# First loads in the order of their use, x modulated in two halves of the channels, first blocks projected over half of the channels in between

## The reference

```python
m = silu(c) @ w_ada + b_ada          # -> shift1, scale1, gate1, shift2, scale2, gate2, 1024 each
h = x * (1 + scale1) + shift1
P = h @ w_in                         # one projection, cut into the inputs of two branches and gates
A = gated_delta_rule(conv(P[...]))   # starts from the state of the last 3 rows
B = rwkv7(token_shift(P[...]))       # starts from the state of the last row
mix = (sigmoid(P_gA) * (A @ p_a) + sigmoid(P_gB) * (B @ p_b)) @ w_o
x = LN(alpha * x + (1 + gate1) * mix)
x = LN(alpha * x + (1 + gate2) * MoE(x * (1 + scale2) + shift2))   # 64 experts, top 8, one shared
```

## Time and profile before

| | |
|---|---|
| median of 3 runs | 1683.13 us (1680.92 to 1695.8) |
| the profiled execution | 1685.42 us |
| its span, first to last instruction | 1683.7 us |
| busy: PE, DVE, ACT, POOL | 1430.7, 581.4, 263.0, 243.8 us |
| mean granted TensorE clock | 0.888 of full speed |
| DMA | 318.39 MB, mean 189 GB/s |

### The profile page before, as it was taken

The page is one execution under the profiler, slowest core; times in us unless marked ns, Lnnn a source line. Parts: engine busy times, 40 slices in busy tenths (PEclk is TensorE's granted clock), DMA queues, the critical chain, the costliest instruction groups (busy, mean ns, idle before and its releaser), DMA issues.

```text
span 1683.7 us, 21034 instructions
## 1 busy us (share of the span) xinstructions
PE 1430.7 (85%) x8007; PEld 930.3 (55%) x8007; DVE 581.4 (35%) x1400; ACT 263.0 (16%) x543; POOL 243.8 (14%) x281
## 2 busy tenths in 40 slices
PE   4889999686848997998898898899998889988866
PEld 1545555584637965975445465555555555555532
DVE  0423476446453334223335422222222122221107
ACT  2121441210011111221002111111111111111100
POOL 5000000030003201500000022212222122222200
PEclk9998899688867998999987999889999898998978
DMA  9364410301021011003334249899999989999854
GB/s 322 105 249 171 150 50 2 79 1 40 11 79 47 1 51 50 1 1 132 129 116 178 90 177 357 306 363 354 346 392 363 351 329 342 392 357 358 314 219 187
DMA packets 105488, 318.39 MB, mean 189 GB/s; under 512 B 22319, under 2 KB 39299, under 8 KB 88234
## 3 DMA queue, kind: packets, MB, share of 16 engines
q1 hardware_dynamic: 90694, 289.01, 46.7%
q0 software_dynamic: 12000, 25.20, 4.6%
q10 hardware_dynamic: 2692, 2.79, 0.5%
HBM read 304.53 MB, written 26.58 MB: 197 GB/s over the span
## 4 chain that ended last, share of the span: by engine, by line
PE 67%; DMA 18%; DVE 8%; issue 2%; SPq 2%; ACT 2%; POOLq 0%; DVEq 0%; POOL 0%; ACTq 0%
DMA MT<-h_rows,slot_ids 14%; PE bank L1928 13%; PE bank L1464 9%; PE bank L1587 5%; PE bank L1938 4%; PE bank L1913 3%; PE bank L1648 3%; PE bank L1837 3%; PE bank L1805 3%; PE bank L1661 3%; PE bank L1658 2%; PE bank L2026 2%; DVE inv L876 2%; DVE ring L876 2%; PE bank L1919 2%
## 5 line engine op out<-in xcount | busy, mean ns | idle before, releaser
L1928 PE MATMUL bank<-ring,MT 128*64 128x256 f32 x2400 | 324.1, 431 | 0.0
L1928 PEld LDWEIGHTS bank<-ring,MT 128*64 128x64 f32 x2400 | 187.6, 156 | 108.4 <-issue 42.1
L1351 DVE SCALAR_TENSOR_TENSOR gate<-zs,slot_gate,bank 128x128 f32<-128x128 f32 x75 | 26.1, 348 | 378.1 <-ACT zs L850 378.1
L1464 PE MATMUL bank<-hT,ring 128*128 128x384 f32 x416 | 146.2, 515 | 7.3 <-DVE hT L876 5.1
L430 POOL DMA_INDIRECT MT<-h_rows,slot_ids x75 | 71.5, 953 | 499.2 <-PE bank L1913 294.1
L1938 PE MATMUL bank<-inv,rwp 128*64 128x512 f32 x600 | 141.5, 592 | 0.4 <-ACT rwp L852 0.4
L1913 PE MATMUL bank<-ident,MT 64*128 64x64 f32 x600 | 82.9, 286 | 59.8 <-DMA MT<-h_rows,slot_ids 59.4
L1464 PEld LDWEIGHTS bank<-hT,ring 128*128 128x128 f32 x416 | 83.7, 203 | 67.4 <-issue 10.8
L1913 PEld LDWEIGHTS bank<-ident,MT 64*128 64x128 f32 x600 | 71.8, 200 | 63.9 <-DMA MT<-h_rows,slot_ids 63.1
L1587 PE MATMUL bank<-hT,ring 128*128 128x384 f32 x256 | 89.6, 510 | 10.3 <-DMA ring<-in_w_in_dram 10.3
L1587 PEld LDWEIGHTS bank<-hT,ring 128*128 128x128 f32 x256 | 50.4, 200 | 44.3 <-DMA ring<-in_w_in_dram 10.4
(11 more groups left out here) (364 smaller groups left out, 1849.1 us busy)
## 6 DMA issues: line engine op xcount, KB each, us to landing
ring<-in_we_gate_dram SPq DMA_DIRECT2D x64, 1024.0 KB, 9.0
ring<-in_we_up_dram SPq DMA_DIRECT2D x64, 1024.0 KB, 11.7
inv<-in_we_down_dram SPq DMA_DIRECT2D x64, 1024.0 KB, 8.0
ring<-in_w_ada_dram SPq DMA_DIRECT2D x12, 2048.0 KB, 14.4
ring<-in_w_in_dram SPq DMA_DIRECT2D x7, 2048.0 KB, 9.2
ring<-y_rows SPq DMA_DIRECT2D x6, 2048.0 KB, 8.1
ring<-in_w_in_dram SPq DMA_DIRECT2D x9, 1024.0 KB, 5.2
xs<-in_x_prompt_dram SPq DMA_DIRECT2D x2, 1024.0 KB, 17.0
```

Source lines behind the costliest of these rows:

```text
L1464: last = mm(bank[4 + n % 4][:, 0:T], ring[:, u, k, tok(c)], hT[:, k, :], start=(k == 0), stop=(k == KC - 1))
L1928: last = mm(b[HS * g:HS * g + HS, 0:DE].rearrange("p (w n) -> p w n", w=2), hgT[:, buf, k, :], gu_ring[:, slot, :, k, tok(g)], start=(k == ...
```

## The change

**Loads.** RING_SEQ begins with w_ada slices 0, 2, 1 (ADA_ORDER), so each half of the channels has its shift and its scale early. SP now issues: ring slots 0 and 1 (w_ada 0 and 2), x, ring slot 2 (w_ada 1), w_ada 3 into `ada_last`, a view of the tile `inv`, then the first w_in slice into slot 0 (waits for the first `modulation`), then the 26 state transfers, then the rest. The ring sees one slice less, so RING_BASE and the slot of each later slice follow from RING_SEQ.

**PE.** The parameters are transposed after the first `modulation`, into bank 5. After two slices and their turns, half 0 of x (channel blocks 0 to 3) is transposed; after the other two slices, half 1. The first three output blocks are projected over channel blocks 0 to 3, with `turn_modulation(3)` after the first of them; then, when `hT` is complete, over blocks 4 to 7, and the fourth block as a whole. The states are transposed behind these four blocks, ahead of w_ada slices 4 and 5.

**DVE.** par first, then for each half its 8 blocks of modT and three pairs of multiply and add (`modulate_half`), then the states. mod_ev counts one more (4 becomes 5).

**ACT.** The wait for past_ev ahead of the projections is gone; PE waits for it at j = 1.

The modulation of the second stage (after the first layer norm) runs through the new helper with the same banks, operations and order.

```diff
...
@@ -271,7 +272,10 @@
         N_ADA1 = 4
-        RING_SEQ = [("ada", i) for i in range(N_ADA1)]
+        ADA_ORDER = [0, 2, 1, 3] + list(range(N_ADA1, N_ADA))
+        RING_SEQ = [("ada", ADA_ORDER[i]) for i in range(N_ADA1 - 1)]
         for i in range(4):
             RING_SEQ += [("in", i), ("ada", N_ADA1 + 2 * i), ("ada", N_ADA1 + 2 * i + 1)]
         RING_SEQ += [("in", i) for i in range(4, 8)]
@@ -279,13 +283,13 @@
         def ring_use(n):
             kind, i = RING_SEQ[n]
-            return ("ada_mm", i + 1) if kind == "ada" else ("proj_mm", [4, 8, 12, 14, 17, 21, 25, 29][i])
+            return ("ada_mm", ADA_ORDER.index(i) + 1) if kind == "ada" else ("proj_mm", [4, 8, 12, 14, 17, 21, 25, 29][i])
         def ada_bank(n):
-            return bank[[3, 4, 6][n % 3] if n < N_ADA1 else n % 3]
-        RING_BASE = [len(range(i, N_ADA + len(RING_IN), RING)) for i in range(RING)]
+            return bank[[3, 4, 0, 3][n] if n < N_ADA1 else n % 3]
+        RING_BASE = [len(range(i, len(RING_SEQ), RING)) for i in range(RING)]
         RING_MG = [RING_BASE[i] + len(range(i, 8, 3)) for i in range(RING)]
         RING_END = [RING_MG[0] + 2, RING_MG[1] + 1, RING_MG[2] + 1]
@@ -485,16 +489,19 @@
                 c0, w = (512 * i, 512) if kind == "ada" else RING_IN[i]
                 load(ring[:, n % RING, :, 0:w], (w_ada_v if kind == "ada" else w_in_v)[:, :, c0:c0 + w], f"ring{n % RING}")
-            for n in range(RING):
+            for n in range(2):
                 ring_load(n)
             load(xs[:, 0:2, :], x_prompt[0].rearrange("(t p) d -> p t d", p=P), "x_in")
             load(xs[:, 2, :], x_sample.rearrange("s t d -> (s t) d"), "x_in")
+            ring_load(2)
+            load(ada_last, w_ada_v[:, :, 512 * 3:512 * 4], "ada_last")
+            ring_load(3)
             for b in range(RB):
                 load(past_r[NSEQ * b:NSEQ * (b + 1), :], state_rwkv_shift[0, :, 0, tok(b)], "past_in")
             for b in range(QB):
                 load(past_q[24 * (b % 4):24 * (b % 4 + 1), b // 4, :],
                      state_gdn_conv[0, :, :, tok(b)].rearrange("s w c -> (s w) c"), "past_in")
-            for n in range(RING, len(RING_SEQ)):
+            for n in range(RING + 1, len(RING_SEQ)):
                 ring_load(n)
@@ -698,7 +705,6 @@
             def mg(q, key):
                 merge_gates(MG_STEPS.get((q, key), []))
-            act.wait_ge(S("past_ev"), 2)
             for n in range(RB):
                 projected(n)
                 if n % 4 == 3 or n == RB - 1:
@@ -904,44 +910,43 @@
             cp(cT[:, :, :], bank[1][:, 0:72].rearrange("p (k r) -> p k r", r=9), "start_ev")
             dve.wait_ge(S("pool_chain"), n_const[0])
             dve.wait_ge(S("start_t"), 2)
-            cp(par[:, :], bank[0][:, 0:130], "start_ev")
-            dve.wait_ge(S("start_t"), 3)
-            cp(rwp[:, :, 1 + SEQ:].rearrange("p b (s t) -> p b s t", s=NSEQ)[:, :, :, 0],
-               bank[2][:, 0:112].rearrange("p (b s) -> p b s", s=NSEQ), "past_ev")
-            qs = qkv[:, :, 3 + SEQ:].rearrange("p b (s t) -> p b s t", s=NSEQ)
-            for w in range(3):
-                cp(qs[:, :, :, w], bank[2][:, 112:400].rearrange("p (b s w) -> p b s w", s=NSEQ, w=3)[:, :, :, w],
-                   "past_ev" if w == 2 else None)
+            cp(par[:, :], bank[5][:, 0:130], "start_ev")
             def mod_blocks(src, b0, b1, plus_one):
                 tt(modT[:, b0:b1, :], src[:, 9 * b0:9 * b1].rearrange("p (b r) -> p b r", r=9),
                    over(par[:, b0:b1], 9), ALU.add)
-                for b in plus_one:
-                    ts(modT[:, b:b + 8, :], modT[:, b:b + 8, :], 1.0, None, ALU.add, name="mod_ev")
-            dve.wait_ge(S("ada_t"), N_ADA1)
-            mod_blocks(bank[5], 0, 16, [8])
-            def modulate(before, shift, scale, banks, tiles=range(TILES)):
-                for i in range(6):
-                    t, k0 = i // 2, 4 * (i % 2)
-                    if t not in tiles:
-                        continue
-                    dve.wait_ge(S("x_turned"), before + i + 1)
-                    src = bank[banks[i]][:, :].rearrange("p (k t) -> p k t", k=4)
-                    out = hT[:, k0:k0 + 4, tok(t)]
-                    sc, sh = modT[:, scale + k0:scale + k0 + 4, :], modT[:, shift + k0:shift + k0 + 4, :]
-                    if t < 2:
-                        sc, sh = over(sc[:, :, 0], P), over(sh[:, :, 0], P)
-                    else:
-                        src, out = [v.rearrange("p k (s t) -> p k s t", s=NSEQ) for v in (src, out)]
-                        sc, sh = [v[:, :, 1:9].unsqueeze(3).broadcast_to([P, 4, NSEQ, LS]) for v in (sc, sh)]
-                    tt(out, src, sc, ALU.mult)
-                    tt(out, out, sh, ALU.add, "hT")
-            modulate(0, 0, 8, [0, 2, 3, 4, 6, 7])
+                for b, n in plus_one:
+                    ts(modT[:, b:b + n, :], modT[:, b:b + n, :], 1.0, None, ALU.add, name="mod_ev")
+            def modulate_half(before, t, k0, shift, scale, b):
+                dve.wait_ge(S("x_turned"), before + 1)
+                src = b[:, :].rearrange("p (k t) -> p k t", k=4)
+                out = hT[:, k0:k0 + 4, tok(t)]
+                sc, sh = modT[:, scale + k0:scale + k0 + 4, :], modT[:, shift + k0:shift + k0 + 4, :]
+                if t < 2:
+                    sc, sh = over(sc[:, :, 0], P), over(sh[:, :, 0], P)
+                else:
+                    src, out = [v.rearrange("p k (s t) -> p k s t", s=NSEQ) for v in (src, out)]
+                    sc, sh = [v[:, :, 1:9].unsqueeze(3).broadcast_to([P, 4, NSEQ, LS]) for v in (sc, sh)]
+                tt(out, src, sc, ALU.mult)
+                tt(out, out, sh, ALU.add, "hT")
+            for half in range(2):
+                dve.wait_ge(S("ada_t"), 2 * half + 2)
+                mod_blocks(bank[1], 4 * half, 4 * half + 4, [])
+                mod_blocks(bank[1], 8 + 4 * half, 12 + 4 * half, [(8 + 4 * half, 4)])
+                for t in range(TILES):
+                    modulate_half(3 * half + t, t, 4 * half, 0, 8, bank[[[2, 7, 6], [2, 7, 0]][half][t]])
+            dve.wait_ge(S("pool_chain"), n_const[0])
+            dve.wait_ge(S("start_t"), 3)
+            cp(rwp[:, :, 1 + SEQ:].rearrange("p b (s t) -> p b s t", s=NSEQ)[:, :, :, 0],
+               bank[0][:, 0:112].rearrange("p (b s) -> p b s", s=NSEQ), "past_ev")
+            qs = qkv[:, :, 3 + SEQ:].rearrange("p b (s t) -> p b s t", s=NSEQ)
+            for w in range(3):
+                cp(qs[:, :, :, w], bank[0][:, 112:400].rearrange("p (b s w) -> p b s w", s=NSEQ, w=3)[:, :, :, w],
+                   "past_ev" if w == 2 else None)
             for b in range(RB):
                 dve.wait_ge(S("proj_ev"), b + 1)
...
@@ -1423,47 +1430,58 @@
                 return u
             def modulation(n, n_ring):
-                u = ring_wait(n_ring)
+                if n_ring is None:
+                    pe.wait_ge(S("ada_last"), 16)
+                    w = ada_last
+                else:
+                    w = ring[:, ring_wait(n_ring)]
                 for k in range(KC):
-                    last = mm(ada_bank(n)[32 * (k % 4):32 * (k % 4) + 9, :], cT[:, k, :], ring[:, u, k, :],
+                    last = mm(ada_bank(n)[32 * (k % 4):32 * (k % 4) + 9, :], cT[:, k, :], w[:, k, :],
                               start=(k < 4), stop=(k >= 4))
                 sig(last, "ada_mm")
             def turn_modulation(n):
                 pe.wait_ge(S("ada_row"), n + 1)
                 for c in range(4):
-                    last = mm(bank[5 if n < N_ADA1 else 3][:, 36 * n + 9 * c:36 * n + 9 * c + 9],
+                    o = 36 * ADA_ORDER[n] + 9 * c
+                    last = mm(bank[1 if n < N_ADA1 else 3][:, o:o + 9],
                               mod_part[:, n % RING, tok(c)], part_sel, start=True, stop=True)
                 sig(last, "ada_t")
-            for n in range(N_ADA1):
-                modulation(n, n)
-                if n:
-                    turn_modulation(n - 1)
-            turn_modulation(N_ADA1 - 1)
-            pe.wait_ge(S("pool_chain"), n_const[0])
+            def turn_x_half(half, banks):
+                for t in range(TILES):
+                    if half:
+                        pe.wait_ge(S("hT"), min(t, 1) + 1)
+                    for k in range(4):
+                        last = tr(bank[banks[t]][:, tok(k)], xs[:, t, (4 * half + k) * P:(4 * half + k + 1) * P],
+                                  ident[:, :])
+                    sig(last, "x_turned")
+            modulation(0, 0)
             pe.wait_ge(S("par_in"), 16 * 8)
-            tr(bank[0][:, 0:110], par_a, ident[0:110, 0:110])
-            sig(tr(bank[0][:, 110:130], par_b, ident[0:20, 0:20]), "start_t")
-            pe.wait_ge(S("past_in"), 16 * (RB + QB))
-            tr(bank[2][:, 0:112], past_r, ident[0:112, 0:112])
-            for a in range(3):
```

(59 more changed lines are left out.)

## The result

The changed kernel takes 1661.42 us (median of 4 runs, 1658.52 to 1667.0) against 1684.96 (4 runs, 1680.92 to 1695.8): ratio 0.9867, 95% interval 0.9822 to 0.9912. Five further rounds gave 0.9848 (0.9804 to 0.9892). So it is faster by 1.3 to 1.5%, some 22 to 26 us, where 16.5 was forecast; it lies just above the low end of the range, and on the other side of the 1% than the case that I had given more. The profiled execution of the changed kernel was the slowest of its four.

A forecast was written before the change was run, and what follows sets the result against it. DMA was taken to bound the first 38 us, then a 21 us serial chain ending in DVE's `hT`. Four blocks done at 65.5 instead of 82.05 gain 16.5: 1683.13 - 16.5 = 1666.6, forecast 1667 us, range 1661 to 1676.

The forecast's parts named there:

- the case that I had given more: Whole kernel: measured time within 1% of the unchanged kernel, chance 0.58, against 0.39 for faster by over 1%.
- What bounds it, and the loads: Start: DMA bounds 38 us, then a 21 us serial chain; third slice at 28.3, w_ada 3 lands 33.9, w_in 39.5.
- PE up to `hT`: Start: slices of 3.60 us and turns of 1.88, x transposed in halves, PE starts projecting at 42.3 us.
- So slices and turns don't speed PE up: Start: PE's slices and turns leave the clock at half, so half clock was taken at 42.3 us.
- The halves: First projection: four matmuls 3.9 us, turn 1.2, eight matmuls beside DVE 5.2, last 20 matmuls 12.9; done at 65.5.
- Rival 1: First projection: the split runs at half clock, four blocks done at 72.5, gain 9.5 us, kernel 1674; chance 0.14.
- The rule against it: First projection: a skill text says waits between bursts send the clock to half and each burst begins slow.
- Behind it: After the four blocks: next w_in slice lands 8.68 us after issue, states' transposes fill idle time, shift reaches the end whole.
- The sum: Whole kernel: median 1683.13 less the start's 16.5 us gives 1666.6, forecast 1667, by its own bounds 1665 to 1669.
- rival 3: Experts' stage: slow-clock stretches, 39 us, grow and take the 16.5 us gain back, up to 1700; chance 0.06.
- Rival 2: Start's loads: x, w_in or w_ada 3 land later than issue order suggests, 5 us at most, kernel 1672; chance 0.13.
- The sign that I had set for being wrong: Start: PE awaiting a load between 30 and 43 us would show the prediction wrong.

The follow-up runs named there:

- e2: The changed kernel with the 26 state transfers issued ahead of w_ada 3 and the first w_in slice again; ratio to the unchanged kernel 0.9881.
- after: The changed kernel as first measured and profiled; median 1661.42 us, profiled span 1665.3 us.
- r1_after: The changed kernel again, no edit, for a second profile; ratio to the unchanged kernel 0.9848, profiled span 1665.2 us.
- r0_before: The unchanged kernel again, no edit, for a second profile; profiled span 1683.3 us.
- e4: The changed kernel with w_in slices 1 and 3 also loaded ahead into the free tile and two turns one block later; ratio to the unchanged kernel 0.9775, median 1652.76 us.
- e1: The changed kernel without projecting over half the channels; the four blocks start when hT is whole; ratio to the unchanged kernel 0.987.
- e3: The unchanged kernel with only the states' loads, transposes and copies moved as in the change; ratio to the unchanged kernel 0.9949.
- e7: The unchanged kernel with one matmul of 80 columns added ahead of the first merge gate; ratio 0.9983, median 1684.07 against 1691.04 us.
- before: The unchanged kernel as first measured and profiled; median 1684.96 us, profiled span 1683.7 us.
- e5: The unchanged kernel with one matmul of 128 columns added ahead of the first merge gate; ratio to the unchanged kernel 0.9942.
- e8: The unchanged kernel with eight matmuls of 128 columns added ahead of the first merge gate; profiled span 1687.9 us.
- e6: The changed kernel with seven matmuls of 128 columns added ahead of the first merge gate; ratio to the unchanged kernel 0.9863.

## Why the prediction was right, and where not

**What bounds it, and the loads: right.** The third slice started at 27.99 (28.3 said), w_ada 3 was not waited for, the w_in slice was waited for until 39.18 (landing 39.5 said). e2 showed the states' 3 us.

**PE up to `hT`: the clock was mis-sized.** "So slices and turns don't speed PE up" was read from the earlier trace rows, which is one execution. The third and fourth slice took 1.90 and 2.95 us in after instead of 3.60, the turn between them 1.03 instead of 1.88. First projection at 39.18, and 41.16 in r1_after, where I had 42.3. The row showed what that execution did, not what the work does: r0_before, with the same program, was at full clock from 21.5 to 24.9 us. With the faster clock PE was there before the w_in slice, so in after that load set the start, not PE. In e4, where both slices took 3.60, it began at 40.45: even there the turn (1.03) and most of the second half of x (1.53 for 2.4) were at full clock.

**The halves: right in form, 1.5 us too dear.** Four matmuls took 2.85 us (3.9 said, half clock assumed for part of it), the turn 0.96 (1.2). From there PE's eight matmuls and DVE's half ran side by side as worked out, 4.8 us by the weight loads and 5.0, with PE waiting 0.51 for DVE, and the last 20 matmuls took 13.2 with their first weight load (12.9 said). Four blocks done at 61.15, 65.5 said: 3.1 us of the miss lie ahead of the first matmul, 1.5 in the first half block and the turn, and the rest took 0.2 longer than said. Rival 1 (half clock through the split) was wrong in sign: in the profiles of after the clock stayed full from 37.6 and 40.8 us through all four blocks, since the split left no wait over 0.51 us in them. The rule against it needs a wait, and met one in e1, unsplit: its projection ran 3.1 us slow behind 5.24 us of waiting.

**Behind it: right in size.** The next group began 9.1 us behind the four blocks (8.7 before). In r1_after PE waited 0.65 us for the load ahead of it, as foreseen. In the profile of after it didn't wait; its second turn ran at half clock until just ahead of 70.25:

```profile
68.33 1.88 PE L1447 MATMUL bank<-MT 105*128 105x9 f32 x8 [1.39 <-ACT MT L645]
```

The states' transposes cost nothing that shows. DVE's mixing began at 63.2 and nobody waited for it.

**The sum: the step that failed is "the shift reaches the end whole, unless something behind it takes it back".** Two things behind it moved, both by the clock. The merge stage, of which the prediction says nothing, added 7.2 us in every profile of after, and so it did in e1, e2, e3 and e4. The experts' stage took 11 and 7 us back: that is rival 3's mechanism, short of the 16.5 us that would have undone the gain. In the profiles this makes 19.9 at the first merge gate, 27.1 behind the merge, 18.2 at the end. The timed ratios say 22 to 26, so the timed executions must have lost less in the experts' stage than the profiled ones, or had other gains; they have no profiles, and it isn't shown.

That 1661.42 lies in the range is in part luck. The range's low end, 1661, stood for 4 us of luck in the experts' stage, which in both profiles went the other way; what brought the time there is a cheaper start, 19 us for 16.5, and the merge stage's clock. That those 7 us are alignment and not a property of the change is shown for profiled executions by e3, which has them without the new order, and e7, which gives them to the kernel before; in timed runs it isn't shown.

**Rival 2**, late loads, did not occur. The sign that I had set for being wrong, a wait for a load between 30 and 43 us, did: PE waited 0.69 us for the w_in slice ahead of 39.18. The slice wasn't late (39.5 said), PE was early. Several of the other places that were to show the steps came early as well: the fourth slice at 33.49 for 36 to 37, the first projection at 39.18 and 41.16 for 42 to 43, the next group at 70.25 and 71.91 for 74 to 75.

## What to carry to other kernels

Ask of a serial start which operand each step needs first, and let the first matmuls run over the half that is ready: here it was worth some 7 us in the trace, 3.1 of them because PE didn't wait and its clock didn't fall. Small transfers issued ahead of large ones cost the large ones 3 to 4 us here, so put them behind the first load on the path. And before a gain of under 1% is trusted or forecast, compare the granted clock stage by stage in two profiles of the same kernel: here one small matmul more, a shift of 0.50 us, went with 7 us less in the merge stage, more than moving the states had gained at the start.

## What the runs showed of the hardware

The clock can fall and rise at the same places of the work in execution after execution: from 108 us ahead of the first merge gate on, the falls and rises of before and r0_before lie at the same places within 0.1 us up to the products with p_a, though their first rises were 32 us apart (53.1 and 21.5 us). It needn't be so: e5, e7 and e8 run the same program up to their added matmuls, and e7 alone had other falls between 111 and 60 us ahead of the gate; from 26 us ahead up to the gate, with the added delay taken off, before, r0_before and these three agree within 0.1.

In the merge stage there were three outcomes for the same stretch of matmuls: 6.8, 17.1 and 20.5 us at 1.2 GHz, with the fall 24.65 to 25.03 us behind the first merge gate (21.4 and 21.5 in e6 and e8), 25.11 to 25.16, and 24.5. Between the first two lies 0.08 us. Work added ahead of the stage made it shorter in e7 and e8.

Slices of 9 rows and their turns were at half clock in one execution and partly at full in the next: 3.60 us in before against 1.90 in after for a slice, 1.88 against 1.03 to 1.06 for a turn. Half-clock time in the experts' stage, 144.9 to 169.6 us, goes with the stage's length, 714.9 to 726.0 us.
